# Seven half-size products in place of eight for three projection chunks, and the last residual half and the first gather in two pieces

## The reference, cut to what matters

```python
h = rms_norm(x, norm1_gain[layer])
proj = jnp.einsum('bsd,dn->bsn', h, w_in[layer])
q_a, k_a, v_a, q_i, k_i, w_i, q_b, k_b, v_b, g_b = jnp.split(proj, cuts, axis=-1)
...
out_a = dsa_attention(q_a, k_a, v_a, q_i, k_i, w_i, rel_bias, topk)   # 64 keys per query by index score
...
q_b = rotary(q_b...); k_b = rotary(k_b...)
y_b = retention(q_b, k_b, v_b)
out_b = jax.nn.silu(g_b) * norm(y_b)
x = x + jnp.einsum('bsm,md->bsd', jnp.concatenate([out_a, out_b], -1), w_out[layer])
h2 = rms_norm(x, norm2_gain[layer])
x = x + moe_ffn(h2, w_router[layer], b_router[layer], w_mlp1[layer], ...)   # top 4 of 32 experts
return rms_norm(x, final_gain)
```

## Time and profile before

| | |
|---|---|
| median of 3 runs | 1078.7 us (1077.63 to 1080.11) |
| profiled execution, its own time | 1080.09 us |
| its span | 1078.3 us |
| TensorE busy | 1040.4 us, 96% |
| VectorE, ScalarE, POOL busy | 265.9, 152.9, 22.2 us |
| DMA moved | 429.87 MB, mean 399 GB/s |

### The profile page before, as it was taken

The page is one execution under the profiler, slowest core; times in us unless marked ns, Lnnn a source line. Parts: engine busy times, 40 slices in busy tenths (PEclk is TensorE's granted clock), DMA queues, the critical chain, the costliest instruction groups (busy, mean ns, idle before and its releaser), DMA issues.

```text
span 1078.3 us, 11417 instructions
## 1 busy us (share of the span) xinstructions
PE 1040.4 (96%) x4628; PEld 399.4 (37%) x4628; DVE 265.9 (25%) x649; ACT 152.9 (14%) x278; POOL 22.2 (2%) x29
## 2 busy tenths in 40 slices
PE   9999999999999999999999999898989899999996
PEld 7458454333333333333333333232323233333331
DVE  2455622422222222222220302121222212120221
ACT  1231322110111110101010111011101101111111
POOL 1212000000000000000000000000000000000000
PEclk9999998999999999999998999999999999999999
DMA  9886957999999999999999999999999999999996
GB/s 330 239 245 269 378 217 266 423 428 421 428 433 430 430 430 430 430 430 432 432 430 430 430 432 433 432 429 434 432 433 432 430 434 430 435 423 434 425 422 246
DMA packets 35376, 429.87 MB, mean 399 GB/s; under 512 B 5164, under 2 KB 6608, under 8 KB 16624
## 3 DMA queue, kind: packets, MB, share of 16 engines
q1 hardware_dynamic: 33424, 426.03, 93.8%
q10 hardware_dynamic: 1216, 1.70, 1.1%
q0 software_dynamic: 704, 1.71, 0.6%
HBM read 426.80 MB, written 2.62 MB: 398 GB/s over the span
## 4 chain that ended last, share of the span: by engine, by line
PE 72%; DMA 26%; SPq 0%; DVE 0%; issue 0%; ACT 0%; DVEq 0%
PE ps L1399 30%; DMA w1r<-w_mlp 24%; PE ps L1429 13%; PE ps L1467 5%; PE ps L1376 4%; PE ps L1126 3%; PE ps L1138 3%; DMA w2r<-w_mlp 2%; PE ps L1193 1%; PE ps L1257 1%; PE ps L1302 1%; PE ps L1158 1%; PE ps L1268 1%; PE ps L1383 1%; PE ps L1407 1%; PE ps L1443 1%
## 5 line engine op out<-in xcount | busy, mean ns | idle before, releaser
L1399 PE MATMUL ps<-w1r,arena 128*64 128x512 f32 x2024 | 478.0, 608 | 21.0 <-DMA w1r<-w_mlp 21.0
L1399 PEld LDWEIGHTS ps<-w1r,arena 128*64 128x64 f32 x2024 | 138.2, 139 | 281.7 <-issue 253.6
L1429 PE MATMUL ps<-w2r,arena 128*64 128x512 f32 x960 | 211.4, 593 | 6.6 <-DMA w2r<-w_mlp 6.6
L1429 PEld LDWEIGHTS ps<-w2r,arena 128*64 128x64 f32 x960 | 68.8, 137 | 145.1 <-issue 135.5
L964 DVE TENSOR_TENSOR arena<-ps,cols 128x512 f32<-128x512 f32 x31 | 21.4, 692 | 277.0 <-PE ps L1383 277.0
L1002 DVE TENSOR_TENSOR arena<-arena 128x512 f32<-128x512 f32 x32 | 22.1, 692 | 163.8 <-ACT arena L618 163.7
L985 DVE TENSOR_SCALAR arena<-small,rank,gate 128x64 f32<-128x64 f32 x128 | 31.3, 308 | 121.4 <-PE ps L1487 121.4
L622 ACT ACTIVATE arena<-ps 128x512 f32<-128x512 f32 x31 | 18.5, 597 | 290.0 <-PE ps L1407 290.0
L1376 PE MATMUL ps<-acc,arena 128*64 128x512 f32 x248 | 58.6, 592 | 0.0
L1467 PE MATMUL ps<-arena 128*128 128x512 f32 x112 | 55.5, 618 | 0.0
L627 ACT ACTIVATE arena<-ps 64x512 f32<-64x512 f32 x29 | 17.1, 591 | 268.2 <-PE ps L1429 268.2
(11 more groups left out here) (261 smaller groups left out, 591.4 us busy)
## 6 DMA issues: line engine op xcount, KB each, us to landing
w1r<-w_mlp SPq DMA_DIRECT2D x46, 4096.0 KB, 30.9
w2r<-w_mlp SPq DMA_DIRECT2D x29, 2048.0 KB, 17.5
w1r<-w_mlp SPq DMA_DIRECT2D x28, 2048.0 KB, 11.6
w2r<-w_mlp SPq DMA_DIRECT2D x14, 4096.0 KB, 21.1
w1r<-w_mlp SPq DMA_DIRECT2D x20, 1024.0 KB, 9.7
w1r<-w_in SPq DMA_DIRECT2D x6, 2048.0 KB, 19.5
w2r<-w_mlp SPq DMA_DIRECT2D x6, 1024.0 KB, 9.8
w1r<-w_out SPq DMA_DIRECT2D x2, 2048.0 KB, 13.4
```

Source lines behind the costliest of these rows:

```text
L1399: ins = mm(ps[64 * c:64 * c + 64, z_bank(base, e) + n, :], hgT[:, par, k % 4, 64 * (k // 4):64 * (k // 4) + 64], cols_z, start=False, stop ...
L1429: ins = mm(ps[at:at + 64, 6, :], actT[:, k % 4, 64 * (k // 4):64 * (k // 4) + 64], w2r[:, k // 2, col:col + 512], start=(k == 0), stop=(k ...
```

## The change

Two parts. In the first, the chunks C_QKB, C_VB and C_GB are multiplied as a 2x2 block product (2 token tiles, 2 halves of the inner dimension, 2 halves of the columns) with seven products of half size and precomputed sums of blocks in place of eight. VectorE makes four sums of `hT` (`xsum`) and the four sums of C_QKB's weights; POOL makes the sums of the weights of C_VB and C_GB (`weight_sums`). ScalarE copies the first product out (`product_out`), and VectorE adds the other six to it in seven operations (`joined`). The norm factor, which was the copy's scale, now goes into the rotary tables, into the retention scores and into the gate. The gate is kept raw in SBUF (`g_raw`) and made later. In the second part, tile 1's second residual half is added and transposed in two pieces of 256 columns, and the first gather is made in two pieces of half the columns each, in the order in which they are transposed. Some semaphores are merged (`tables_in`, `late_in`, `one_ready`).

```diff
+            a11, a12, a21, a22 = (hT[:, k:k + 4, n:n + P] for n in (0, P) for k in (0, 4))
+            s1, s2, s3, s4 = xsum
+            link(v.tensor_tensor(s1, a21, a22, ALU.add))
+            v.tensor_tensor(s3, a11, a21, ALU.subtract)
+            link(v.tensor_tensor(s2, s1, a11, ALU.subtract))
+            v.tensor_tensor(s4, a12, s2, ALU.subtract).then_inc(sums_scaled, 1)
...
+            dve.wait_ge(win_in[C_QKB], 16)
+            for j, (to, a, b) in enumerate(((t3, b22, b12), (b12, b12, b11), (t2, b22, b12), (t4, t2, b21))):
+                v.tensor_tensor(to, a, b, ALU.subtract).then_inc(sums_scaled, 1)
+                dve.wait_ge(sums_scaled, j + 2)
...
+            def joined(to, c, banks, done):
+                c11, c12, c21, c22 = (to[:, t, n:n + 256] for t in range(TT) for n in (0, 256))
+                dve.wait_ge(products, base + 6)
+                dve.wait_ge(done, 1)
+                v.tensor_tensor(c12, c11, p6, ALU.add).then_inc(done, 1)
+                v.tensor_tensor(c11, c11, p2, ALU.add).then_inc(done, 1)
...
+                dve.wait_ge(proj_done, c + 2)
+                v.tensor_tensor(c12, c12, p3, ALU.add).then_inc(done, 1)
...
             for t in range(TT):
                 dve.wait_ge(g_exp, t + 1)
...
-                v.scalar_tensor_tensor(gb[:, t, :], ps[:, t, :], st[:, 6 + t:7 + t], gb[:, t, :], ALU.mult, ALU.mult).then_inc(g_silu, 1)
-                v.tensor_tensor(sT[:, h, :], ps[:, 4 + h, 0:KW], dec[:, h, :], ALU.mult).then_inc(sT_sb, 1)
+                link(v.scalar_tensor_tensor(gb[:, t, :], g_raw[:, t, :], st[:, 6 + t:7 + t], gb[:, t, :], ALU.mult, ALU.mult))
...
+            def last_residual():
+                dve.wait_ge(out_mm, 4)
+                for q in range(2):
+                    sl = acc[:, 1, 512 + 256 * q:768 + 256 * q]
+                    v.tensor_tensor(sl, ps[:, 3, 256 * q:256 * q + 256], sl, ALU.add).then_inc(x2_ready, 1)
...
+            def seven(c, banks, sums, count, between=None, ready=None):
+                for i, (a, b, made) in enumerate(((a11, b11, 0), (a12, b21, 0), (s3, t3, 1), (s1, b12, 2), (s2, t2, 3), (a22, t4, 4), (s4, b22, 4))):
+                    if made:
+                        pe.wait_ge(sums, count + made)
+                    if ready is not None and i % 2 == 0 and ready[i // 2] is not None:
+                        pe.wait_ge(*ready[i // 2])
+                    for k in range(4):
+                        ins = mm(ps[:, banks[i // 2], 256 * (i % 2):256 * (i % 2) + 256], a[:, k, :], b[:, k, :], start=(k == 0), stop=(k == 3))
+                    ins.then_inc(products if i < 6 else proj_done, 1)
+                    if between is not None and i in between:
+                        index_scores(between.index(i))
...
-            for t in range(TT):
-                for k in range(KD):
-                    ins = mm(ps[:, t, :], hT[:, k, P * t:P * t + P], win[C_QKB][:, k, :], start=(k == 0), stop=(k == KD - 1))
-                    if k % 4 == 1:
-                        index_scores(2 * t + k // 4)
-            chunk(C_VB, 2, by_token)
+            seven(C_QKB, QKB_BANKS, sums_scaled, 1, between=(0, 2, 4, 5))
+            seven(C_VB, VB_BANKS, w_sums, 0, ready=((idx_relu, 3), (idx_relu, 3), (idx_relu, 4), (idx_relu, 4)))
             pe.wait_ge(rotated, 2)
...
-            chunk(C_GB, 0, by_token)
+            seven(C_GB, GB_BANKS, w_sums, 4, ready=(None, (row_sb, 1), (qkbT_sb, 1), (qkbT_sb, 2)))
...
+            pe.wait_ge(gb_sb, 8)
             chunk(C_QA, 2, by_head)
...
-                for c in range(2):
-                    ins = mm(ps[64 * c:64 * c + 64, 0, :], onehotP[:, 0, t, :], acc[:, t, 512 * c:512 * c + 512],
+                for i in range(2):
+                    for c in range(2):
+                        x2_cols = acc[:, t, 512 * c:512 * c + 512].rearrange("p (q j) -> p j q", j=4)[:, 2 * i:2 * i + 2, :]
+                        ins = mm(ps[64 * c:64 * c + 64, i, 0:256], onehotP[:, 0, t, :], x2_cols, start=(t == 0), stop=(t == TT - 1))
```

More of the change, by code:

```diff
@@ L510, in _, with product_out @@
                           relT[0:AH, :].rearrange("h (a r) -> h a r", a=1).to_broadcast((AH, P, REL))).then_inc(relT_out, 16)
+            def product_out(to, c, banks, done):
+                act.wait_ge(products, 6 * (c - C_QKB) + 2)
+                nc.scalar.activation(to[:, 0, 0:256], ps[:, banks[0], 0:256], ACT.Copy).then_inc(done, 1)
             for j in range(4):
+                if j == 1:
+                    product_out(qkb, C_QKB, QKB_BANKS, qkb_sb)
                 act.wait_ge(idx_mm, j + 1)
@@ L774, in _ @@
                 dve.wait_ge(idx_added, h + 1)
+            joined(qkb, C_QKB, QKB_BANKS, qkb_sb)
             link(v.memset(score[0:64, P - CH:P], NEG))
@@ L803, in _ @@
             ins.then_inc(late_consts, 1)
+            joined(g_raw, C_GB, GB_BANKS, gb_sb)
+            dve.wait_ge(dec_in, 16)
+            for h in range(BH):
+                dve.wait_ge(ret_s, h // 2 + 1)
+                v.scalar_tensor_tensor(sT[:, h, 0:S], ps[:, 4 + h, 0:S], st[:, 6:7], dec[:, h, 0:S], ALU.mult, ALU.mult)
+                v.scalar_tensor_tensor(sT[:, h, S:KW], ps[:, 4 + h, S:KW], st[:, 7:8], dec[:, h, S:KW], ALU.mult, ALU.mult).then_inc(sT_sb, 1)
             for t in range(TT):
@@ L889, in x2T_out, with last_x2T_out @@
                 v.tensor_copy(x2T[:, 4:8, P * t:P * t + P], ps[:, 5, :].rearrange("p (k n) -> p k n", k=4)).then_inc(x2T_dve, 1)
+            def last_x2T_out():
+                for q in range(2):
+                    dve.wait_ge(x2_tr, 4 + q)
+                    v.tensor_copy(x2T[:, 4 + 2 * q:6 + 2 * q, P:S],
+                                  ps[:, 5 + 2 * q, 0:256].rearrange("p (k n) -> p k n", k=2)).then_inc(x2T_dve, 1)
             def choose(t):
@@ L925, in _ @@
             choose(0)
-            residual(1, 1)
+            last_residual()
+            last_x2T_out()
             place(0, rank_mm, 1)
-            x2T_out(1)
             norm2(1)
@@ L1127, in one_tile @@
                 return ins
-            def by_token(w, bank, n):
-                for t in range(TT):
-                    ins = one_tile(w, bank, n, t)
-                return ins
             def by_head(w, bank):
@@ L1312, in x2_T, with last_x2_T @@
                 ins.then_inc(x2_tr, 1)
+            def last_x2_T(q):
+                pe.wait_ge(x2_ready, 4 + q)
+                if q == 0:
+                    pe.wait_ge(x2T_dve, 1)
+                for k in range(2):
+                    ins = nc.tensor.transpose(ps[:, 5 + 2 * q, P * k:P * k + P], acc[:, 1, P * (4 + 2 * q + k):P * (4 + 2 * q + k) + P], ident)
+                ins.then_inc(x2_tr, 1)
             def route(t):
@@ L1349, in _ @@
             x2_T(1, 0)
+            last_x2_T(0)
             pe.wait_ge(rank_in, 32)
```

153 lines of the change are left out of this document (92 added, 61 removed).

## The result

The changed kernel takes 1080.33 us (median of 14 runs, 1079.72 to 1082.53), the kernel before 1077.42 us beside it (14 runs, 1076.43 to 1080.11). The ratio is 1.0029, with a 95% interval of 1.0022 to 1.0036: slower by 2.9 us, where the forecast was 1073.9 and faster. 1080.33 lies within 0.4 us of rival 1's point, but that point was counted from 1078.7: it stood for +2.0 us, and +2.9 was measured.

A forecast was written before the change was run, and what follows sets the result against it. TensorE's front was taken to set when the expert weight stream starts. Products -4.4 and last residual -0.4 gave -4.8 us, from 1078.7 to 1073.9 us; range 1072.0 to 1080.8.

The forecast's parts named there:

- rival 1: Front: VectorE's index adds and POOL's sums block each other; TensorE stands still 5.2 us, 1080.7 us; chance 0.22.
- What bounds the kernel: Expert weight stream starts when TensorE's front ends; a microsecond of matmul saved there is one of the kernel.
- Products: C_QKB, C_VB, C_GB: seven half-size products save 1.47 us a chunk, -4.4 us in all.
- Sums for C_VB and C_GB: Eight POOL weight sums at 2.5 us each, 20 us from 27.4 us; POOL free at 47.4 us.
- Joining C_QKB: VectorE's additions done at 48.1 us, `rotated` at 56.0; rotary work hidden with 1.3 us to spare.
- Rival 2: Front: only POOL gives way, or its sums are slower than priced; 2.5 us wait, 1076.4 us; chance 0.12.
- I take nothing: Gather: no cost for columns four apart, since 0.84 ns a column leaves the reads time.
- Rival 3: Gather by columns four apart is slow; doubling 1.88 and 1.71 us costs 3.6 us, 1077.5 us; chance 0.10.
- The last residual: Routing: residual add in two pieces lets the router end at 166.9 instead of 167.3 us, -0.4 us.
- The sum: -4.4 - 0.4 = -4.8 us, from the median 1078.7 to 1073.9 us.
- The base: Profiled execution 1080.09 us, 1.4 us above the runs' median; forecast counted from the median 1078.7.

The follow-up runs named there:

- run 1: The kernel before, unchanged, profiled once more (one execution): 1076.51 us.
- run 7: Kernel before plus the seven products alone, weight sums of C_VB and C_GB on VectorE instead of POOL: 1072.62 us, ratio 0.9959.
- run 11: The changed kernel once more, unaltered, against the kernel before: 1080.05 us, ratio 1.0021.
- run 10: The changed kernel with first-gather pieces of columns side by side instead of four apart: 1078.96 us, ratio to the kernel before 1.0007.
- run 5: Kernel before plus eight unused POOL subtractions of 1024 columns that read SBUF (one execution): 1079.66 us.
- run 2: Kernel before plus the seven products alone, weight sums on POOL, residual and gather as before: 1078.80 us, ratio 1.0016.
- run 9: The changed kernel with weight sums of C_VB and C_GB moved to VectorE, gather still strided: 1073.83 us, ratio to the kernel before 0.9966.
- run 8: The changed kernel with those weight sums on VectorE and the old gather: 1073.02 us, ratio to the kernel before 0.9962.
- run 3: Kernel before plus the second part alone, last residual and first gather in pieces: 1078.49 us, ratio 1.0011.
- run 4: Kernel before plus only the last residual half and its transposes in two pieces, old gather: 1076.70 us, ratio 0.9994.

## Why the prediction was wrong

**What bounds the kernel: right.** From the stream's first load to the end of the execution it is 903.4 us before (176.74 to 1080.09), 903.2 after (176.57 to 1079.72), 902.9 in run 1 and 903.4 in run 7. A microsecond of the front is one of the kernel, in both directions, but not to a tenth: over all thirteen profiles this last part takes 902.5 to 904.4 us, the longest in runs 11 and 10 (904.0 and 904.4).

**Products: right.** -4.4 us were forecast; run 7, which has them with the cover restored, gives -4.7 (-3.0 to -5.9), and its front is 4.85 us shorter by the rows. C_GB's 56 instructions take 12.09 us there, 12.26 by the forecast, and C_QA starts at 71.90 where 72.4 was forecast.

**Sums for C_VB and C_GB: the price was right, 2.35 for 2.5 us. The step that failed is the next, "Joining C_QKB", which says that the rotary work is hidden with 1.3 us to spare.** It took VectorE's index adds to last what they did before, although POOL's sums now ran beside them. Run 5 shows that they don't, without the products; run 7 shows that the loss goes when POOL's sums go. In the changed kernel the joining ends 5.1 us after its forecast time, `rotated` comes at 61.1 instead of 56.0, and of the delay 3.7 us become a standstill. The sum from run 7's C_QA at 71.90 to the changed kernel's at 77.98 closes so: 3.72 us of wait, 0.54 that TensorE is late at the end of C_VB already (57.45 against 56.91), and 1.82 of half clock after it (transposes 1.41 for 0.95, the row 0.85 for 0.43, C_GB 13.03 for 12.09), 6.08 in all. The wait and the part of the clock make up for each other between executions: run 11 waited 4.24 us and had C_GB in 12.41, and its front is as long to 0.05 us.

**Rival 1 was what happened, but not in its own detail.** It gave 5.2 us of standstill and up to 3.2 for the clock; it was 3.7 and 1.8. It had VectorE's index adds get in by pairs, the first at 32.2 us. They got in one for each sum and began at 39.14, because the scalings of the rotary tables and the multiplications L830 before them were held as well, four of the six for about a POOL sum each; once in, the adds took 11.61 us, since POOL had ended at 46.3 us. And its condition, a wait over 4.8 us, was wrong: run 2 loses 1.7 us with a wait of 4.20, as the clock behind a wait costs too. Rival 2, that only POOL gives way, is refuted: POOL's sums kept 2.35 to 2.42 us.

The Trainium skill says in SBUF — State Buffer, section Who interferes with whom, that a VectorE instruction with two SBUF inputs contends with a GpSimd one that reads and not with one that only writes, and that copies and `tensor_scalar` can take the shared port pair as well, in a mode that their operands must allow, and then contend with GpSimd. The traces agree on VectorE's side: up to 2.64 us beside reads, 351 and 480 ns beside memsets (two instructions), and 1.12 us instead of 0.35 for `tensor_scalar` beside memsets (one instruction). On POOL's side they agree only in part. In run 7 its first rotary operation took 2.18 us instead of 1.27 when it met a VectorE sum under way. But in the changed kernel POOL's sums start 2.43 us apart while adds get in that last 0.35 to 0.49 us when nothing holds them; that is 0.08 us more than a sum lasts, and the rotary operations, which meet no such add, have a gap of 0.07 us too. How the adds get in is not shown. I had put the first half at 0.22 and not read the second against L821 and L830.

**The gather: the step "I take nothing" for columns four apart failed.** Rival 3's mechanism was on: the gathers nearly doubled, in the timelines from 1.08 to 2.00 and 2.01 us. Its price was mis-sized, because it doubled 1.88 and 1.71 us, durations at half clock: it gave 3.6 us, the table gives 1.5 for the new gather against the old, and the medians 0.6 (runs 9 and 8) and 1.8 (3 and 4); for the step alone it gives 1.7, the medians 1.1 (11 and 10). The argument that 0.84 ns a column leaves the reads time is refuted, and it used the wrong row: a gather of 4 instructions x 512 columns in 1.08 us takes 0.53 ns a column, and 0.98 four apart.

The rule on 16-byte lines in the Trainium skill (SBUF — State Buffer, section Door 1: The DMA port swizzle), that each access in a new line pays, agrees; its size here is a factor of 1.85. The same passage gives 4 fp32 as how far one can stride for free; a step of 4 fp32 is not free here. No run tried another step, so that the lines of 16 bytes are the reason is not shown, only that the step is.

**The last residual: right in direction, half the size.** -0.4 was forecast. Run 4's medians give -0.4 with zero in the interval, which alone shows nothing; the rows give -0.2, in run 4 and in run 8.

**The sum.** Products -4.7 (run 7), meeting of the engines +6.4 (run 2's +1.7 less run 7's -4.7), residual -0.4, gather +0.6 to +1.8: +1.9 to +3.1 where +2.9 and +2.5 were measured. By the rows it is +1.1 for the front and +1.3 for the routing, +2.4; the rest of the +2.9 is not taken apart. Rivals 1 and 3 came together; the forecast priced each alone and gave neither the sum of the two, which lies above its range's end at the sizes that it gave them. That 1080.33 still fell inside the range is luck: the range was counted from 1078.7, the median of three runs, and the fourteen beside the result give 1077.42. From 1078.7 a loss of 2.9 us would have been 1081.6, outside.

**The base.** The profiled execution was 1.4 us above its median, and I took that as the runs' spread. Run 1 places it: one fall of the clock at 167.5 us, in the stretch whose rows priced the gather, makes 2.4 us of the 3.6 between the two executions, the start before C_QI 0.8, and the part behind the first load 0.5. Runs 7, 8 and 9 (1072.62, 1073.02 and 1073.83 us) beat both kernels.

## What to carry to other kernels

Before work is put on an idle GpSimd, list what VectorE runs in the same microseconds with SBUF operands: those instructions can wait for a whole GpSimd operation each, and a cover has to be counted with them so. Here the same eight sums fitted into VectorE's own gaps, at half the duration, and TensorE waited for none of them. And price a stretch from a profile only after comparing its granted clock with a second execution's: a duration at half clock hides both the gaps and what an instruction takes at full clock.

## What was unexpected in the hardware

- Small operations pay the full price of the exclusion: a 128x32 scaling by a constant per partition took up to 2.37 us beside POOL's sums (four in 0.67 us without them).

```profile
L821 DVE TENSOR_SCALAR w2r<-w2r,st x4: 228/1225/2365, 29.6 to 34.2; 128x32 f32<-128x32 f32 x4
```

- POOL hardly suffers: its eight operations took 19.57 us in run 5, 2.45 each with their gaps, and a sum by itself lasts 2.35. It did wait where VectorE was in first (6.23 for 5.31 us in run 7).
- TensorE's moving operand at every fourth float costs 2.00 us instead of 1.08 for eight float32 instructions of 256 columns.
- The same program shows a granted clock of 0.50 or 1.00 between 168 and 174 us in different executions (1080.09 and 1076.51 us). What decides it stays open.
